# Value rings of twelve pages in the sample attention, and the closing products cut at 304, 288, 288 and 176 tokens

## The reference, cut to what matters

```
u = RMSNorm(h);  [q_a|kv_a|q_idx|k_idx|w_idx|q_b|k_b|v_b|g_a|g_b] = u @ w_in
A: index scores over the causal prefix, top 256 keys, grouped softmax attention over them
B: (softmax(Q1 K1^T/8) - lambda softmax(Q2 K2^T/8)) V, RMSNorm per head
merged = sigmoid(g_a) * (A @ w_br_a) + sigmoid(g_b) * (B @ w_br_b)
h += RMSNorm(merged @ w_out)
h += RMSNorm((silu(h' @ w_gate) * (h' @ w_up)) @ w_down),  h' = RMSNorm(h), inner width 2816
h += sigmoid(h @ w_ple_gate) * (p @ w_ple_proj)
```

## Time and profile before

| | us |
|---|---|
| median of 3 runs (3669.53 to 3682.44) | 3674.64 |
| the profiled execution's own time | 3671.66 |
| its span | 3670.1 |
| outside the span | 1.6 |
| `sample_select` | about 1091 to 1622 |
| `sample_attend` | about 1622 to 3419 |
| `tail` | 3419 to 3670 |

### The profile page before, as it was taken

The page is one execution under the profiler, slowest core; times in us unless marked ns, Lnnn a source line. Parts: engine busy times, 40 slices in busy tenths (PEclk is TensorE's granted clock), DMA queues, the critical chain, the costliest instruction groups (busy, mean ns, idle before and its releaser), DMA issues. The chain is left out here.

```text
span 3670.1 us, 69563 instructions
## 1 busy us (share of the span) xinstructions
PE 2985.0 (81%) x26553; PEld 2081.3 (57%) x26553; DVE 1547.9 (42%) x3004; ACT 587.1 (16%) x1294; POOL 589.5 (16%) x1089
## 2 busy tenths in 40 slices
PE   8999899548959688647698988888778989878697
PEld 4444366336749588644465655555545555545596
DVE  2222389837743677543643332253444333102211
ACT  1111210026634200000110110010111010101101
POOL 0000000000002000000023333333342334341000
PEclk9999699859979899878799998988988999889898
DMA  5232312140027344356789998999887989664695
GB/s 193 85 99 81 105 58 77 55 130 1 1 62 231 95 132 133 106 162 188 215 267 303 296 285 267 290 305 295 278 288 230 305 267 302 186 205 123 160 264 153
DMA packets 734994, 667.90 MB, mean 182 GB/s; under 512 B 69850, under 2 KB 607610, under 8 KB 734555
## 3 DMA queue, kind: packets, MB, share of 16 engines
q1 hardware_dynamic: 672730, 479.06, 43.7%
q0 software_dynamic: 61952, 184.62, 15.0%
HBM read 616.52 MB, written 46.98 MB: 181 GB/s over the span
## 5 line engine op out<-in xcount | busy, mean ns | idle before, releaser
L975 PE MATMUL sa_t<-tw_z,tw_w 128*128 128x352 f32 x1664 | 546.4, 484 | 19.0 <-DVE tw_x L1069 10.1
L1808 DVE STREAM_TRANSPOSE sa_key_b<-sa_ring_k 128x2048 f32<-128x2048 f32 x128 | 294.3, 2306 | 456.4 <-PE sa_s L1647 244.7
L1573 POOL DMA_DIRECT2D sa_ring_v<-cache_b_kv x512 | 275.6, 538 | 1097.2 <-PE sa_o L1714 738.6
L975 PEld LDWEIGHTS sa_t<-tw_z,tw_w 128*128 128x128 f32 x1664 | 323.7, 199 | 213.0 <-issue 55.6
L975 PE MATMUL sa_t<-tw_x,tw_w 128*128 128x352 f32 x960 | 310.4, 483 | 53.1 <-DMA tw_w<-w_br_a 45.7
L213 PE MATMUL pr_acc<-pr_w,pr_u_t 128*128 128x512 f32 (+1 forms) x864 | 326.6, 539 | 0.0
L1574 POOL DMA_DIRECT2D sa_ring_va<-cache_a_kv x512 | 275.0, 537 | 53.7 <-issue 24.9
L975 PEld LDWEIGHTS sa_t<-tw_x,tw_w 128*128 128x128 f32 x960 | 188.6, 200 | 163.5 <-issue 68.6
L213 PEld LDWEIGHTS pr_acc<-pr_w,pr_u_t 128*128 128x128 f32 x864 | 152.2, 190 | 167.9 <-issue 167.9
L1647 PE MATMUL sa_s<-sa_key_b,sa_q_pad 32*32 32x256 f32 x8192 | 195.7, 423 | 45.1 <-DVE sa_key_b L1808 41.3
L439 PE MATMUL sel_g<-sel_u,sel_gw 128*128 128x352 f32 x768 | 228.8, 461 | 0.0
(11 more groups left out here) (358 smaller groups left out, 3673.2 us busy)
## 6 DMA issues: line engine op xcount, KB each, us to landing
sa_ring_k<-cache_b_kv SPq DMA_DIRECT2D x512, 256.0 KB
sa_ring_v<-cache_b_kv POOLq DMA_DIRECT2D x512, 256.0 KB, 6.0
tw_w<-w_gate_up SPq DMA_DIRECT2D x88, 512.0 KB, 8.3
sa_ring_ka<-cache_a_kv SPq DMA_DIRECT2D x512, 64.0 KB
sa_ring_va<-cache_a_kv POOLq DMA_DIRECT2D x512, 64.0 KB, 5.6
tx_w<-w_gate_up SPq DMA_DIRECT2D x44, 512.0 KB
tp_w<-w_gate_up SPq DMA_DIRECT2D x44, 512.0 KB, 4.9
tw_w<-w_down SPq DMA_DIRECT2D x32, 512.0 KB, 6.4
```

What stands on the lines that cost most here:

```text
L975: ins = pe.matmul(bank[:, 0:self.width], self.w[:, at % self.SLOTS, k - lo, :], moving[:, k, :], start=(k == 0), stop=(k == kc - 1))
L1573: pool.dma_start(ring_v[:, n % RING, :], rows_of(cache_b, page, 1)).then_inc(v_in[n // 4 % 2], 16)
L1808: nc.vector.transpose(key_b[:, at:at + 4].rearrange("p g n s -> p (g n s)"), ring_k[:, at:at + 4, :].rearrange("p g e -> p (g e)")).then_i ...
```

## The change

`FIRST, SECOND` become 304 and 576. The pieces are then 304 tokens in `sample_select`, 288 and 288 in `sample_attend`, and 1056 - 880 = 176 in `tail`. The value rings of both branches have 12 pages instead of 8, and three semaphores each in place of two, one for each group of four pages; the key rings stay as they are.

```diff
-FIRST, SECOND = 216, 704
+FIRST, SECOND = 304, 576
...
-    RING, RING_A = CH, 2 * CH
+    RING, RING_A, RING_V = CH, 2 * CH, 12
...
-        ring_v = ph.sb("ring_v", [P, RING, H_B * P])
+        ring_v = ph.sb("ring_v", [P, RING_V, H_B * P])
...
-        ring_va = ph.sb("ring_va", [P, RING, P])
+        ring_va = ph.sb("ring_va", [P, RING_V, P])
...
+        v_in, va_in = ([ph.sem(f"{n}{c}") for c in range(3)] for n in ("v_in", "va_in"))
...
-                if n >= RING:
-                    pool.wait_ge(v_used, n - RING + 1)
+                if n >= RING_V:
+                    pool.wait_ge(v_used, n - RING_V + 1)
                 page = pool.value_load(pages[0:1, n:n + 1])
-                pool.dma_start(ring_v[:, n % RING, :], rows_of(cache_b, page, 1)).then_inc(v_in[n // 4 % 2], 16)
+                pool.dma_start(ring_v[:, n % RING_V, :], rows_of(cache_b, page, 1)).then_inc(v_in[n // 4 % 3], 16)
...
-                pe.wait_ge(v_in[part], (v + 1) * 64)
-                pe.wait_ge(va_in[part], (v + 1) * 64)
+                four = 2 * v + part
+                pe.wait_ge(v_in[four % 3], (four // 3 + 1) * 64)
+                pe.wait_ge(va_in[four % 3], (four // 3 + 1) * 64)
```

More of the change, by code:

```diff
@@ L1494, in sample_attend @@
         pages_in, small_in, sel_in = ph.sem("pages_in"), ph.sem("small_in"), ph.sem("sel_in")
-        k_in, ka_in, v_in, va_in = ([ph.sem(f"{n}{c}") for c in range(2)] for n in ("k_in", "ka_in", "v_in", "va_in"))
+        k_in, ka_in = ([ph.sem(f"{n}{c}") for c in range(2)] for n in ("k_in", "ka_in"))
+        v_in, va_in = ([ph.sem(f"{n}{c}") for c in range(3)] for n in ("v_in", "va_in"))
         turned_b, turned_a, scored, a_scored, b_read, a_read = (
@@ L1569, in _ @@
             for n in range(CHUNKS * CH):
-                if n >= RING:
-                    pool.wait_ge(v_used, n - RING + 1)
+                if n >= RING_V:
+                    pool.wait_ge(v_used, n - RING_V + 1)
                 page = pool.value_load(pages[0:1, n:n + 1])
-                pool.dma_start(ring_v[:, n % RING, :], rows_of(cache_b, page, 1)).then_inc(v_in[n // 4 % 2], 16)
-                pool.dma_start(ring_va[:, n % RING, :], rows_of(cache_a, page, 1)).then_inc(va_in[n // 4 % 2], 16)
+                pool.dma_start(ring_v[:, n % RING_V, :], rows_of(cache_b, page, 1)).then_inc(v_in[n // 4 % 3], 16)
+                pool.dma_start(ring_va[:, n % RING_V, :], rows_of(cache_a, page, 1)).then_inc(va_in[n // 4 % 3], 16)
         @block.sync
@@ L1709, in values @@
                         at = 32 * h + 8 * j
-                        pe.matmul(o_bank[32 * h:32 * h + 8, 0:P], prob_t[:, g, 0, at:at + 8], ring_v[:, g, h * P:(h + 1) * P],
+                        pe.matmul(o_bank[32 * h:32 * h + 8, 0:P], prob_t[:, g, 0, at:at + 8], ring_v[:, (v * CH + g) % RING_V, h * P:(h + 1) * P],
                                   start=False, stop=False, tile_position=(0, 32 * h), skip_group_check=True)
@@ L1713, in values @@
                     g = 4 * part + i
-                    pe.matmul(o_bank[32 * i:32 * i + 32, P:2 * P], prob_t[:, g, 1, 32 * j:32 * j + 32], ring_va[:, g, :],
+                    pe.matmul(o_bank[32 * i:32 * i + 32, P:2 * P], prob_t[:, g, 1, 32 * j:32 * j + 32], ring_va[:, (v * CH + g) % RING_V, :],
                               start=False, stop=False, tile_position=(0, 32 * i), skip_group_check=True).then_inc(v_used, 1)
```

## The result

The changed kernel takes 3701.06 us (median of 5 runs, 3693.09 to 3715.33) against 3674.64: a ratio of 1.0078, 95% interval 1.0046 to 1.0110. It is 0.8% slower; 3646 was forecast, a ratio of 0.992. The profiled execution took 3693.1 us where before's took 3671.7, and the stages tell where the 21.4 us are.

What follows compares the result with a forecast made beforehand. Attention was held to lie between TensorE and the DMA, other stages set by TensorE. Selection +86, tail +46, attention -160 gave -28 us on 3671.66, so 3644, forecast as 3646; own range 3615 to 3680, 8 in 10 3592 to 3705.

Steps and rivals of the forecast that it cites:

- Prices of the products: TensorE's time an instruction, interpolated: 0.258 us at 304 tokens, 0.245 at 288, 0.151 at 176.
- Selection and tail: Wider pieces lengthen both: selection +86 us (bounds +60 and +115), tail +46 us (bounds +35 and +52).
- the 14 counted: Selection: 14 us of TensorE's 82.9 us of waits for the count go as fifteen rounds get longer products.
- Last part: Attention's last 182 us: -17 us from narrower products, -21 of 30.6 us of value waits; sum -38.
- rival 4: Attention: value waits come from DMA latency, not ring size; the middle's waits double; kernel 3688 us; chance 0.10.
- The stated bound of -55: Attention's last 182 us: the larger gain allowed, beside a forecast of -38 us and a smaller bound of -17.
- Behind it: Attention's final 87 us: -11 us from narrower products and -2 from a norm, sum -13.
- Middle: Attention's 1273 us of joint key and value loads become DMA-bound at 1190 us: -83, bounds 0 and -156.
- the 306 GB/s: Attention's middle: load rate held over 150 us before, taken as the rule, putting 364 MB at 1190 us.
- rival 2: TensorE sets the pace throughout; the attention's middle reaches 1117 to 1140 us, 320 to 326 GB/s; kernel 3586 us; chance 0.15.
- Rival 1: Attention's middle stays at 286 GB/s as value loads delay keys; kernel 3730 us, break-even at 299 GB/s; chance 0.22.
- Start: Attention's start to 1877 us: -21 products, -4 input, -3 norms, +2 for `n1` and `n2` sharing a step; sum -26 us.

Runs made afterwards that it cites:

- experiment 7: Kernel before with pieces 304, 288, 288, 176, value rings of 8 pages, attention's units ordered by costs at 352 tokens: 3717.5 us, ratio 1.0118.
- experiment 6: Changed kernel with the attention's units in the old order, planner costs taken at 352 tokens: 3677.81 us, ratio 1.0000 to the kernel before.
- experiment 3: Changed kernel with pieces 304, 224, 224, 304, so less TensorE work in the attention: 3807.39 us, ratio 1.0374 to the kernel before.
- experiment 4: Changed kernel loading only half of each of branch B's value pages from the 13th on: 3602.93 us, ratio 0.9821 to the kernel before.
- experiment 5: Changed kernel with pieces 304, 224, 224, 304 and branch B's key ring also at 12 pages: 3801.55 us, ratio 1.0335 to the kernel before.
- experiment 10: Kernel before with pieces 192, 364, 364, 136, rings of 8 pages, `y_t` in the buffer of the squares: 3645.64 us, ratio 0.9910.
- experiment 11: Changed kernel with pieces 248, 312, 312, 184, order taken at 364 tokens, `y_t` in the squares' buffer: 3631.2 us, ratio 0.9886 to the kernel before.
- experiment 8: Kernel before with only the attention's unit order changed, planner counting 364 tokens for 352: 3662.33 us, ratio 0.9961.
- experiment 9: Changed kernel with the attention's unit order taken at 364 tokens: 3661.24 us, ratio 0.9959 to the kernel before.
- experiment 1: Changed kernel's pieces (304, 288, 288, 176) with value rings of 8 pages as in the kernel before: 3737.61 us, ratio 1.0192.

## Why the prediction was wrong

**Prices of the products, right.** 0.258 and 0.245 us an instruction came out as interpolated, and so did 0.151 in the tail (704 instructions in 106.72 us).

**Selection and tail, right.** +85.6 for +86, +39.1 for +46. The waits for the count swallowed 12.6 us, close to the 14 counted. A token costs 85.6/88 = 0.97 us in the selection and 39.1/40 = 0.98 in the tail. The tail at 176 tokens took between 287.8 and 295.6 us in the runs, so its price is good to some 0.1.

**Last part, the sum right by luck.** -35.1 was measured for -38. The ring does take the value waits away where the 13.3 us of a `dn` run had to cover a page's issue and landing, and rival 4 falls. But by experiments 7 and 6 the three steps are 180.7 to 173.7 (pieces, -7 for the -17 forecast, since TensorE's waits for values grow from 30.6 to 37.3 us), to 136.5 (ring, -37 for -21) and to 145.6 (order, +9, not forecast). The errors cancel. The stated bound of -55 does not come out of the terms either: -17 and all of the 30.6 make -48. Behind it -13.2 for -13.

**Middle, wrong in one term: the rate.** The step "I take 1190, since a deeper ring and earlier free buffers make such stretches the rule" failed. The mechanism, loads and not TensorE, is shown by experiments 3, 4 and 5; the 306 GB/s was mis-sized, and 297 was measured: 1218.9 us where 1190 was forecast. Through every kernel here with products narrower than before's and all its bytes the middle ran at 292 to 300 GB/s. The 306 was the mean of 150 us in which TensorE was busy for 137; the stage has stretches in which less is asked for. Windows of 50 us of the kernel after:

```profile
2715.00:2765.00 50.00, 42.94 (x775) 31.46 (x747) 19.68 (x15) 7.12 (x16) 17.13 (x32) 0.91 1.01 322
2765.00:2815.00 50.00, 20.35 (x469) 12.96 (x469) 23.24 (x39) 6.70 (x13) 17.13 (x32) 0.70 0.74 243
2815.00:2865.00 50.00, 33.74 (x395) 24.20 (x394) 25.21 (x41) 11.05 (x18) 17.13 (x32) 0.79 0.80 253
...
2965.00:3015.00 50.00, 45.41 (x852) 33.03 (x851) 19.96 (x33) 9.49 (x14) 23.96 (x46) 1.00 1.07 342
3015.00:3065.00 50.00, 33.78 (x383) 25.09 (x379) 14.75 (x17) 3.06 (x6) 13.20 (x26) 0.83 0.70 218
```

Of the 24 such windows from 1965 to 3165 us eight reach 320 or more and five are under 270; before, of the 23 from 1965 to 3115 us, three and six. The change did make fast stretches more frequent, and the slow ones pulled the mean down. The two around 2800 us hold the second piece's norms, with TensorE busy 20.35 us of 50. The one at 3015 falls into two parts (SPq is SyncE's queue):

```profile
3015.00:3034.00 19.00, 5.34 (x26) 3.90 (x21) 6.62 (x6) 0.00 (x0) 8.18 (x16) 0.74 1.04 323
3034.00:3065.00 31.00, 28.44 (x358) 21.19 (x358) 8.14 (x11) 3.06 (x6) 5.02 (x10) 0.89 0.49 154
...
3036.02 19.94 SPq L898 DMA_DIRECT2D tw_w<-w_gate_up  x3
3056.56 0.35 SPq L1586 DMA_DIRECT2D sa_ring_k<-cache_b_kv  x1
...
3058.15 0.54 POOL L1574 DMA_DIRECT2D sa_ring_v<-cache_b_kv  x1 [29.15 <-PE sa_o L1716]
```

First the DMA is dense and the engines wait for it. Then TensorE works (busy 28.44 of 31 us) and little is asked for, since the buffers are full: GpSimd stands 29 us for a free value page, and SyncE 20 us at weight loads whose slots TensorE has not freed. The key ring is full too until VectorE has turned its next half at 3052.1 us; the key loads follow at 3056.6, behind the weight loads. So the 297 is a mean of stretches that the loads bound and stretches in which full buffers wait for TensorE, and not a ceiling of the DMA; 97 us less work on TensorE (experiment 3) shortened the whole by only 10.6 us. The same table reads the share: 0.93 at 297 and 1.07 at 342 both come to some 3.13 thousandths for each GB/s, so by these rows a share of 1 is about 320 GB/s (estimate), and 306 would have asked for 0.96 as the mean of 1190 us.

The Trainium skill (DMA: Bandwidth & Descriptors, Specifications) gives about 358 GB/s for HBM to one core. The densest 50 us after came to 342, under it, and 15 us at 2780 to 361, about it; no middle of any run passed 300, so rival 2, which rested on more than 320 throughout, falls with experiment 3.

**Rival 1** named the mechanism that came: waits pass from values to keys. It decides "from the rate", with "break-even at 299", which is a middle of 1218 us; 1218.9 came. By its own sum the kernel would then have been as fast as before. Its rate of 286 did not come, nor its 3730.

**Start, wrong.** Forecast -26, measured -2.6. Two terms failed. "+2 because the planner now puts `n1` and `n2` into one step ahead of the key transposes" measured 13.2 (experiment 6 against after). And "384 instructions x 0.0536 = -21" counted all products as lying on the path, while the first part stands on loads: the scores of the first chunk begin 77.7 us into the phase before and 76.7 after, and TensorE's longest wait for `w_br_a` is 24.6 us before, 26.1 after (38.4 and 39.8 in all). In the old order the start fell by 15.8 us (experiment 6) where 28 were forecast without the "+2"; the new order then took 13.2 of them back.

**What it adds up to.** With only the middle wrong (28 us short) the change would have come out at the time of before; the 23 us of the start made it slower. The middle's miss takes away the gain, and the start's makes the loss, as experiment 6 shows from the other side: ratio 1.0000 without the new order. The measured 3701.06 lies near the far end of the stated range, 3592 to 3705, which was widened for rivals; the forecast's own range, 3615 to 3680, does not hold it.

**Selection against attention.** The prediction found the sum of TensorE's work to be zero and asked where it is on the path. The runs give the answer as a price: 0.97 and 0.98 us a token outside the attention; in the attention, 86.0/128 = 0.67 with eight pages in the old order and 64.6/128 = 0.50 where the narrower pieces bring the new one, and with twelve pages 41.2/128 = 0.32 from 288 to 224 (experiment 3, whose order of units is that of its own width; its tail took 155.2/128 = 1.21 a token from 176 to 304). Work in the attention is the cheaper, so the pieces were moved the wrong way; experiments 10 and 11 move them back and win 19 and 27 us by the ratios at the same order (against 8 and 9).

**Left open.** Why the middle's gaps remain when both rings are deeper and TensorE has time (experiment 5): the four weight slots are as before in every run, and key loads stand behind weight loads in SyncE's queue in every run; neither was changed. And how much of an order's effect is chance of alignment: experiment 9 gained 19 us in the middle and gave back 6 in the start, although its first norms stand where they do in 6. Twelve pages with 352 tokens did not run, so the ring's worth at the old widths is not shown.

## What to carry to other kernels

When work is moved between stages, price it in each stage by what sets that stage's end: a stage near a second limit gives back only the part down to that limit, while a stage without one charges for nearly all of it. Take a stage's rate from its mean with its gaps, or from its whole length in a run that is plainly bound by it, never from its best stretch; waits that move from one buffer to another at an unchanged rate show that the engines' waits are not what sets it. Where widths feed a planner, compare the orders it gives before reading anything into the widths, and hold the order fixed in one run.

## What was not expected of the hardware

- The middle stays at 296 to 300 GB/s (DMA share 0.93 to 0.94) in eight kernels with TensorE busy from 877 to 1019 us of it, rings of 8 or 12 (the ninth, experiment 1, has 292), while single windows of 50 us pass 340.
- Removing 400 us of VectorE's waits for pages changed the attention by 0.6 us and its middle by 11.6 (experiments 3 and 5).
- The order of the same instructions, with the same bytes and the same tiles, moves the kernel by 0.4 to 1.2% (experiments 6, 8 and 9).
- What a stand of TensorE costs behind it: 128 score matmuls took 4.53 us at 1889.6 us of the kernel after, behind the wait of 15 us, and 2.76 us at 1787.8. The granted clock was 0.50 from 1885 to 1890 us, the lower of its two levels (1.2 GHz), and 1.00 from 1785 to 1791, the higher (2.4 GHz). The window around the stand has a mean of 0.67:

```profile
1860.00:1910.00 50.00, 23.48 (x454) 16.04 (x456) 35.32 (x47) 6.12 (x12) 10.27 (x20) 0.67 0.57 179
```
